# Chosen-key logits as half-height products in pairs, masks from one signed comparison, scores in 512-key units

## The reference, cut to what matters

```python
for each block of 128 queries (tile t, keys 0 .. 128*(t+1)-1):
    rel   = relu(einsum('bqjd,bkd->bqjk', qi_blk, k_idx))     # 8 index heads of width 64
    score = einsum('bqjk,bqj->bqk', rel, wi_blk)              # one score for each query and key
    _, sel = lax.top_k(score, 256)                            # 256 keys for each query, ties to the lower key
    logits = einsum('bqhd,bqnd->bhqn', q_blk, k[sel]) * 64 ** -0.5   # 4 heads of width 64, one shared k
    p = softmax(logits);  out = einsum('bhqn,bqnd->bqhd', p, v[sel])
```

## Time and profile before

| | us |
|---|---|
| median of 3 runs | 2766.08 (2763.96 to 2767.02) |
| profiled execution, time / span of the core | 2757.8 / 2756.1 |
| TensorE busy | 2467.8 (90%) |
| VectorE busy | 1202.4 (44%) |
| ScalarE busy | 914.0 (33%) |
[...]

### The profile page before, as it was taken

How to read it: one execution, slowest core, us unless ns; L and a number is a source line. 1 busy time by engine, 2 the same in 40 slices (tenths; PEclk the granted TensorE clock), 3 DMA queues, 4 the chain that set the end, 5 groups by cost and what they waited for, 6 DMA issues and landing times.

```text
span 2756.1 us, 30251 instructions
## 1 busy us (share of the span) xinstructions
PE 2467.8 (90%) x10376; PEld 1394.6 (51%) x10392; DVE 1202.4 (44%) x2802; ACT 914.0 (33%) x1882; POOL 186.3 (7%) x370
## 2 busy tenths in 40 slices
PE   6999789789999789999589996997899996999994
PEld 3565334555665444444345643455566553444442
DVE  3434468875542411111333426789655333111115
ACT  2131379554531111111122215794545211111113
POOL 0000031000000000000200001310000000000002
PEclk9999999999999889999789999999999997999996
DMA  6100001401000389999511000013010005999975
GB/s 237 43 31 25 31 13 51 120 2 47 1 11 39 148 319 359 368 364 370 195 42 52 7 25 34 19 55 107 1 47 1 26 31 230 342 360 370 366 282 206
DMA packets 105713, 370.54 MB, mean 134 GB/s; under 512 B 20759, under 2 KB 40173, under 8 KB 81005
## 3 DMA queue, kind: packets, MB, share of 16 engines
q1 hardware_dynamic: 91760, 318.54, 32.2%
q0 software_dynamic: 13824, 50.34, 4.7%
HBM read 304.42 MB, written 64.30 MB: 134 GB/s over the span
## 4 chain that ended last, share of the span: by engine, by line
PE 70%; DVE 13%; issue 8%; ACT 6%; DMA 1%; PEldq 1%; PEld 1%; POOL 1%; DVEq 0%; ACTq 0%; SPq 0%; POOLq 0%
PE bank L1191 16%; PE bank L762 9%; PE bank L1208 8%; PE bank L1116 8%; PE bank L842 5%; PE bank L751 5%; PE bank L765 5%; PE bank L874 4%; ACT group_arena L1466 3%; ACT heads_cols L1458 2%; DVE residual L2259 1%; DVE softmax_stats L1761 1%; PE bank L1045 1%; PE bank L1177 1%; PE bank L1183 1%
## 5 line engine op out<-in xcount | busy, mean ns | idle before, releaser
L762 PE MATMUL bank<-w_ring,normed_cols 128*128 128x260 f32 (+4 forms) x1280 | 433.5, 491 | 5.2 <-ACT heads_cols L1491 3.3
L762 PEld LDWEIGHTS bank<-w_ring,normed_cols 128*128 128x128 f32 x1280 | 237.1, 191 | 173.2 <-issue 154.3
L765 PE MATMUL bank<-normed_cols,w_ring 128*128 128x512 f32 x640 | 283.2, 602 | 7.4 <-ACT group_arena L1368 6.5
L751 PE MATMUL bank<-ident,group_arena 128*128 128x128 f32 (+1 forms) x1200 | 186.8, 298 | 114.2 <-DVE group_arena L1689 92.6
L1208 PE MATMUL bank<-heads_cols,group_arena 128*128 128x512 f32 x512 | 231.8, 595 | 2.8 <-DVE group_arena L2219 2.8
L1191 PE MATMUL bank<-w_ring,group_arena 128*128 128x512 f32 x512 | 229.8, 602 | 3.5 <-issue 1.8
L751 PEld LDWEIGHTS bank<-ident,group_arena 128*128 128x128 f32 (+1 forms) x1200 | 143.7, 150 | 170.1 <-issue 92.5
L1116 PE MATMUL bank<-w_ring,heads_cols 128*128 128x512 f32 x512 | 225.5, 595 | 2.0 <-DVEq L252 2.0
L1191 PE MATMUL bank<-normed_cols,group_arena 128*128 128x512 f32 x512 | 225.0, 592 | 0.0
L765 PEld LDWEIGHTS bank<-normed_cols,w_ring 128*128 128x128 f32 x640 | 122.5, 194 | 160.7 <-issue 152.0
L2219 DVE COPY group_arena<-bank 128x256 f32<-128x256 f32 x64 | 27.2, 424 | 395.4 <-PE bank L1198 395.4
(11 more groups left out here) (322 smaller groups left out, 3070.5 us busy)
## 6 DMA issues: line engine op xcount, KB each, us to landing
heads_cols<-in_expert_w_down SPq DMA_DIRECT2D x64, 1024.0 KB, 9.2
w_ring<-in_expert_w_gate SPq DMA_DIRECT2D x32, 1024.0 KB, 10.0
w_ring<-in_expert_w_up SPq DMA_DIRECT2D x32, 1024.0 KB, 14.4
normed_cols<-in_expert_w_gate SPq DMA_DIRECT2D x32, 1024.0 KB, 10.4
normed_cols<-in_expert_w_up SPq DMA_DIRECT2D x32, 1024.0 KB, 15.5
expert_rows<-group_arena SPq DMA_DIRECT2D x64, 512.0 KB, 9.3
w_ring<-in_w_in SPq DMA_DIRECT2D x6, 2048.0 KB, 9.1
expert_rows<-heads_cols SPq DMA_DIRECT2D x1, 8192.0 KB, 27.7
```

The costliest lines, as they stand in the source:

```text
L751: last = pe.transpose(bank(4 + r % 2)[0:rows, col:col + src.shape[0]], src, ident[0:src.shape[0], 0:src.shape[0]])
L762: m = pe.matmul(out[:, 0:width], HT[:, k, part * P:(part + 1) * P], w, start=(k == 0), stop=(k == K - 1))
L765: m = pe.matmul(out[0:width, :], w, HT[:, k, part * HALF:(part + 1) * HALF], start=(k == 0), stop=(k == K - 1))
```

## The change

1. `logits` for sparse attention becomes `logits_by_pair`: heads 2i and 2i+1 are multiplied together, each on its own 64 rows. For tiles 0 to 3 both lie in one bank group; for tiles 4 to 7 they take both groups, and TensorE waits for both. The second unit of a pair issues no logits.
2. `kTd_odd` goes, and with it GpSimd's three operations on keys and TensorE's wait for them.
3. `pick` starts from a sign of score minus threshold that ScalarE computes (`compare`), with its sum; VectorE marks ties (16-bit), ranks them by a scan, corrects a limit, and one operation makes `dropped(t)`, 0 or 1, which a diagonal of negative numbers `ident_neg` adds to the logits. Tile 2 is picked before the attention, and tile t+3 rather than t+2 at tile t.
4. The maximum is negated by the reduction; the scales of the logits move into the copies of q.
5. Scoring goes in 40 units of up to 512 keys, both heads of a pair at once, in alternating bank groups and halves of `rel`; the start of the search is cut into `search_count` and `search_flip`, the second one unit later. Later projections get two steps for each slot below tile 7. Of tile 7's trials still 18 are in the slots, of the `put_later` now 5 there (3 before) and 18 in rounds.

```diff
-        LATER_STEPS = [1 if t >= 4 else 2 for t, _ in SLOTS]
-        WIDEST_SLOTS = [slot for slot in range(4, len(SLOTS)) if slot not in (18, 22)]
-        WIDEST_ROUNDS = [0, 1, 2, 4] + list(range(7, 25, 2))
-        LATER_ROUNDS = [n for n in range(3, 31) if n not in WIDEST_ROUNDS]
+        UNITS = [(t, pair, c0, min(c0 + HALF, (t + 1) * P)) for t, pair in SLOTS for c0 in range(0, (t + 1) * P, HALF)]
+        LATER_STEPS = [1 if t == T - 1 else 2 for t, _ in SLOTS]
+        WIDEST_SLOTS = [slot for slot in range(5, len(SLOTS)) if slot != 22]
+        LATER_ROUNDS = [2, 3, 5, 7, 9, 12, 14, 16, 18, 20, 22] + list(range(24, 31))
+        WIDEST_ROUNDS = [n for n in range(24) if n not in LATER_ROUNDS]
...
+                    def logits_by_pair(u):
+                        _, t, heads, _ = units[u]
+                        sets = [lg.next() for _ in range(2 // len(heads))]
+                        if t >= 2 and heads[0] == 0:
+                            pe.wait_ge(mask_ready, t - 1)
+                        if sets[-1] >= 2:
+                            pe.wait_ge(lg_taken, sets[-1] - 1)
+                        outs = [PS[n % 2] for n in sets] if len(sets) == 2 else [PS[sets[0] % 2][:, i * HALF:] for i in range(2)]
+                        chunks = [(c0, min(c0 + HALF, (t + 1) * P)) for c0 in range(0, (t + 1) * P, HALF)]
+                        ts = slice(t * P, (t + 1) * P)
+                        for c0, c1 in chunks:
+                            for i, L in enumerate(outs):
+                                rows = slice(i * HD, (i + 1) * HD)
+                                pe.matmul(L[:, c0:c1], qTd[rows, heads[0] // 2, ts], kTd[rows, c0:c1], start=True,
+                                          stop=t < 2 and c1 <= t * P)
+                        for i, L in enumerate(outs):
+                            if t < 2:
+                                m = pe.matmul(L[:, ts], ident_h[:, :], masks_h[:, 0, :], start=False, stop=True)
+                            else:
+                                for c0, c1 in chunks:
+                                    m = pe.matmul(L[:, c0:c1], ident_neg[:, :], dropped(t)[:, c0:c1], start=False, stop=True)
+                            if len(sets) == 2 or i == 1:
+                                m.then_inc(lg_ready, 1)
...
-                        if kind == "dsa" and t >= 2 and heads[0] == 0:
-                            pe.wait_ge(mask_ready, t - 1)
+                        if kind == "dsa":
+                            if heads[0] % 2 == 0:
+                                logits_by_pair(u)
+                            return
...
+                def index_unit(u):
+
+                    t, pair, c0, c1 = UNITS[u]
                     n = lg.next()
...
+                    if n >= 2:
+                        pe.wait_ge(lg_taken, n - 1)
+                    for i in range(2):
+                        m = pe.matmul(PS[n % 2][:, i * HALF:i * HALF + c1 - c0],
+                                      qTi[i * 64:i * 64 + 64, pair, t * P:(t + 1) * P],
+                                      kTi[i * 64:i * 64 + 64, c0:c1], start=True, stop=True)
+                    m.then_inc(lg_ready, 1)
...
+                def relu_unit(u):
+
+                    _, _, c0, c1 = UNITS[u]
+                    n = lg.next()
+                    at, w = (n % 2) * HALF, c1 - c0
+                    act.wait_ge(lg_ready, n + 1)
+                    if n >= 2:
+                        act.wait_ge(rel_taken, n - 1)
+                    act.activation(rel[:, :, at:at + w], PS[n % 2][:, :].rearrange("p (i c) -> p i c", i=2)[:, :, 0:w],
+                                   ACT.Relu).then_inc(rel_ready, 1)
...
+                def compare(t):
+
+                    w = (t + 1) * P
+                    if t >= 4:
+                        act.wait_ge(mask_ready, t - 3)
+                    act.activation(pick_sign[:, t % 2, 0:w], scores[:, S_OFF[t]:S_OFF[t] + w], ACT.Sign,
+                                   bias=trial_bias[:, t - 2:t - 1], scale=SIGN_SCALE,
+                                   accum_out=thr[:, 0, t - 2:t - 1]).then_inc(signs_ready, 1)
+
                 def gates_and_squares(t, h):
 
+                    if t < T - 4 and h == 1:
+                        compare(t + 4)
...
-                            chain(dve.tensor_reduce(stats(tile, heads[0], m, 0), src, AX_X, ALU.max))
-                            dve.tensor_scalar(stats(tile, heads[0], m, 1), stats(tile, heads[0], m, 0), -KINDS[kind]["scale"],
-                                              None, ALU.mult).then_inc(max_ready, 1)
+                            dve.tensor_reduce(stats(tile, heads[0], m, 1), src, AX_X, ALU.max, negate=True).then_inc(max_ready, 1)
...
+                for u, (t, pair, _, c1) in enumerate(UNITS):
+                    score(u)
+                    if pair == IDX_HEADS // 2 - 1 and c1 == (t + 1) * P:
+                        finish_row(t)
+                        search_count(t)
+                    if pair == 0 and UNITS[u - 1][0] == t + 1:
+                        search_flip(t + 1)
+                search_flip(2)
...
-                chain(dve.memset(ones_row, 1.0))
+
+                chain(dve.tensor_scalar(trial_bias[:, 0:T - 2], cur, -SIGN_SCALE, None, ALU.mult))
+                dve.sem_inc(thresholds_set, 1)
...
-                        chain(dve.tensor_scalar(a, s, th, 0.0, ALU.is_gt, ALU.add, accum_out=above))
-                        chain(dve.tensor_scalar(s, s, th, None, ALU.is_equal))
+                        dve.wait_ge(signs_ready, t - 1)
+                        chain(dve.tensor_scalar(tie, sgn, 0.0, None, ALU.is_equal))
                     if part == 1:
-                        chain(dve.tensor_tensor_scan(b, ones_row[:, 0:w], s, 0.0, ALU.mult, ALU.add))
-                        chain(dve.tensor_scalar(left, above, -1.0, float(TOPK), ALU.mult, ALU.add))
+                        chain(dve.tensor_tensor_scan(rank, ones[:, 0:1].to_broadcast([P, w]), tie, 0.0, ALU.mult, ALU.add))
                     if part == 2:
-                        chain(dve.scalar_tensor_tensor(b, b, left, s, ALU.is_le, ALU.mult))
-                        chain(dve.tensor_tensor(a, a, b, ALU.add))
+                        chain(dve.tensor_tensor(left, rank[:, w - 1:w], excess, ALU.subtract))
+                        chain(dve.tensor_scalar(left, left, 0.5, float(TOPK - w // 2), ALU.mult, ALU.add))
                     if part == 3:
-                        dve.tensor_scalar(chosen(t), a, -NEG, NEG, ALU.mult, ALU.add).then_inc(mask_ready, 1)
+                        dve.scalar_tensor_tensor(dropped(t), rank, left, sgn, ALU.is_gt, ALU.is_gt).then_inc(mask_ready, 1)
```

More of the change, by code:

```diff
@@ L345, in trunk @@
         kTd = g(14336, SEQ)
-        kTd_odd = g(15360, SEQ)
         qTi = g(0, 4, SEQ)
@@ L1436, in _ @@
                     for half in range(2):
-                        take(copy_to(qTd[:, b, half * HALF:(half + 1) * HALF]))
+                        take(copy_to(qTd[:, b, half * HALF:(half + 1) * HALF], scale=HD ** -0.5))
                 for which in range(2):
@@ L1494, in _ @@
                 i = 0
-                for slot in range(len(SLOTS)):
-                    relu_pair(slot)
+                for u, (t, pair, _, c1) in enumerate(UNITS):
+                    relu_unit(u)
+                    if c1 < (t + 1) * P:
+                        continue
+                    slot = SLOTS.index((t, pair))
                     done = sum(LATER_STEPS[:slot])
@@ L1543, in gates_and_squares @@
                         act.activation(rstd2[:, :], rstd2[:, :], ACT.Sqrt).then_inc(root_ready, 1)
+                act.wait_ge(thresholds_set, 1)
+                for t in range(2, 4):
+                    compare(t)
                 attend("dsa", extra=gates_and_squares)
@@ L1553, in take_q_k @@
                 def take_q_k(t):
-                    take(copy_to(qTm[0:DQ, :, t * P:(t + 1) * P], rows=DQ))
+                    take(copy_to(qTm[0:DQ, :, t * P:(t + 1) * P], rows=DQ, scale=DQ ** -0.5))
                     take(copy_to(kTm[0:DQ, :, t * P:(t + 1) * P], rows=DQ))
@@ L2066, in _ @@
                     dve.wait_ge(stage_out[i], 16 * N_STAGED // 4)
+                for part in range(4):
+                    pick(2, part)
                 attend("dsa", extra=pick_and_norm)
```

165 lines of the change are left out of this document (65 added, 100 removed).

## The result

The changed kernel takes 2785.09 us (median of 4 runs, 2784.7 to 2787.21), the kernel before 2766.55 (4 runs, 2763.96 to 2769.36). The ratio is 1.0067, 95% interval 1.0053 to 1.0082: 18.5 us slower. Forecast was 2788, and slower with a chance of 0.71.

What follows compares the result with a forecast made beforehand. TensorE bounds the two other attentions, ScalarE the search, the order of waits scoring and sparse attention. -4.2 - 0.6 - 0.4 + 9.8 + 6.6 - 0.3 = +10.9 a layer, +21.8 on 2757.8, plus 8.3: 2788 us; range 2757 to 2802.

Steps and rivals of the forecast that it cites:

- Scoring: Scoring stage: alternating banks end TensorE and ScalarE's turn-taking; earlier first trial, shorter trial stretch and tail; -4.2 us a layer.
- the rival: Scoring nears VectorE's bound because GpSimd decides quicker; stage under 85 us, -6 a layer overall, 2754 us, chance 0.18.
- Search: Search stage: one `put_later` less on ScalarE, -0.6 us a layer (0 to -1).
- Masks and maxima up to tile 5's opening: Sparse attention's early tiles, VectorE the limit: cheaper picks bring tile 5's opening to 558.9, -0.4 us a layer (-3 to +3).
- Joint logits: Sparse attention, tiles 5 to 7: cheaper products, but pairs need both bank groups, nothing computed ahead; +9.8 us a layer (+4 to +13).
- half clock: Sparse attention: TensorE's granted clock drops behind its pauses before pairs' logits; four pairs at 1.65 us, +6.6 us a layer.
- Rest: Two other attentions follow TensorE, so their shorter maxima give only the first units; -0.3 us a layer.
- no half clock: Sparse attention: TensorE's pauses slightly shorter than thought, so no slow clock; +4.3 us a layer, 2775 us, chance 0.17.
- Faster: Scoring near VectorE's bound, -11 us a layer; attention +5 without the clock's cost; -6 a layer, 2754 us, chance 0.18.
- Gain and loss cancel: Whole kernel: no net change within 5.5 us (0.2%), 2766 us, chance 0.10.
- Signs change tables: ScalarE in sparse attention: each of four signs costs up to two table loads; +5 us a layer on top, 2798, chance 0.05.

Runs made afterwards that it cites:

- e7: Changed kernel plus 32 unread products of 128 columns into the outputs' bank before each pair's logits from tile 4 on: 2760.59 us, 0.9998 of the kernel before.
- e5: Changed kernel with the kernel before's logits put back (full height, one head at a time, keys split by GpSimd): 2724.81 us, 0.9871 of the kernel before.
- e10: Changed kernel with ScalarE's squares for both heads of a pair moved behind the second exponential: 2772.97 us, 1.0024 of the kernel before.
- e6: e5 with the old maxima, VectorE negating each maximum in an instruction of its own: 2727.74 us, 0.9878 of the kernel before.
- e4: Changed kernel plus nine unread 512-column products into a transposes' bank before pairs' logits from tile 4's second pair on: 2781.72 us, 1.0053 of the kernel before.
- e1: Changed kernel with pairs kept only for tiles 0 to 3, later heads' half-height logits issued singly into their own bank group: 2741.2 us, 0.9907 of the kernel before.

## Why the prediction was right

The sign and the main cause were right. The sizes, per layer (predicted, then measured in the traces; e7's and e5's where named):

- **Scoring, -4.2 and -7.4.** (The three terms given add up to -4.1.) The step that failed is the pace of the trials. The first trial was placed at 332.5 and came at 332.78. But 64.7 us were taken from first to last, and it was 60.8. I had taken GpSimd's decision between two trials as a fixed pace, though I had put "the decisions become quicker when the rows are split" into the rival. The decision itself did not become quicker (its four instructions take 1.5 us on average before and 1.6 after, from 334 to 400 us); what became shorter is GpSimd's wait for ScalarE's next trial, 2.1 us before and 1.7 after. I take it that less stands ahead of the trials in ScalarE's order; that was not tried by itself. The rival's mark of 85 us was not reached (87.7).
- **Search, -0.6 and -0.6.** As predicted.
- **Masks and maxima up to tile 5's opening, -0.4 and +2.1.** The opening came at 553.42 in place of 559.29, 5.9 earlier, where scoring and search alone give 8.0. Up to tile 4's logits the forecast held: counted without these 8.0 they came at 541.2 (533.22 in the trace), and 542.0 was forecast, with the sign of tile 7 and two table loads of 1.28 us ahead of them. The step that failed is tile 4's first pair. From its opening to the next I had 9.7 us, and it was 12.2; the second pair took 8.0 for 7.2. Two things lie in that first pair, and no run separates them (it takes 12.4 us in e7 and 12.1 in e10). It opens after a pause of 5.79 us, and the granted clock behind is 0.52 (533.22 to 537.90), with logits of 2.50 us where the second pair's take 1.35. And the second head's maximum, ready to start when the masks end at 536.9, stands in VectorE's order behind a step that waits for the forgetting sums from ScalarE:

```profile
542.05 0.43 DVE L2041 TENSOR_SCALAR group_arena<-group_arena 128x1024 f16<-128x1024 f16 x1 [1.87 <-ACT forget L1530]
...
542.51 0.83 DVE L1789 TENSOR_REDUCE softmax_stats<-bank 128x1 f32<-128x640 f32 x1
...
545.41 1.35 PE L831 MATMUL bank<-group_arena 64*128 64x512 f32 x8 [1.51 <-ACTq L1367]
```

  The kernel before has the same wait, but there it holds up one head and not a pair. This term was also hiding something: with the pairs gone (e5) the same masks and maxima bring 4.9 us up to tile 5's opening (546.34) and 3.4 behind it, 8.3 in all (16.3 less scoring and search). VectorE was the limit of tiles 4 and 5, as the prediction said, but the joint logits put another wait in its place, so that nothing of the relief was left.
- **Joint logits, +9.8, and half clock, +6.6: 16.4 together, and 20.5** from tile 5's opening to the last values. The joint part is right where the clock is full. In e7 both pairs of tile 5 took 17.8 us (17.4 predicted), both of tile 6 19.1 (19.4), the first of tile 7 9.35 (9.4), and the rest to the last values 19.7 where it was 18.9 before (0.8 more, as predicted): +9.8 in sum. What was mis-sized is the clock. No run shows the +6.6 that the sum has for it, which was my estimate of four pairs at 1.65 us; in its place the runs showed +10.7 by the same rows (tile 5 20.95 to 17.8, tile 6 22.3 to 19.1, tile 7's first pair 12.17 to 9.35, the rest 21.2 to 19.7). Three of the four pairs (the second of tile 5, both of tile 6) cost 1.57 to 1.64, but tile 7's first cost 2.8, and two that I did not count, tile 5's first and tile 7's last, cost 1.6 and 1.5: behind each of the six openings, after pauses of 2.1 to 3.0 us, some products were slow (behind 553.42 the values took 2.21 us for 20, where they take 1.31 in e7 at a granted clock of 1.00).
- **Rest, -0.3 and about -1.8.** The attention ended 14.7 us later and the out projection began 12.9 later (822.91 for 810.05). The difference lies in the two other attentions, 155.5 us long where they were 157.3; the old maxima (e6) give 0.5 of it back, the remainder was not tried.

Sum: +10.9 predicted and +12.8 measured, against 12.9 at the out projection in the trace; 21.8 for two layers against 27.3 between the two traces. The medians differ by 18.5. The 8.3 us that I added for the distance of the profiled execution from its median applied to the kernel before and not to the changed one. So it was partly luck that the forecast of 2788 came within 3 us: sums too small by 5.5 and an offset too large by 8.3 went against each other.

The rivals: *no half clock* is refuted by the windows of 0.69 and 0.58. Its condition, pauses a little shorter than thought, would not have been enough: in e10 pauses of 1.86 and 2.01 us are followed by granted clocks of 0.66 and 0.72, and one of 2.04 by 1.00. *Faster* came halfway with its scoring (-7.4, between the forecast's -4.2 and its -11), but its attention of +5 without the clock's cost was not seen: with filler (e7) scoring and search at -8.0 and the attention at +12.1 leave the yardstick 4.1 above the kernel before's. *Gain and loss cancel* is out by 18.5 us against its 5.5. *Signs change tables* is refuted: the sign at 526.66 has no table load ahead of it, the load at 528.04 belongs to the logarithm of the forget gates and the one at 530.29 to the exponential after it. Between the loads at 506.87 and 528.04 the trace has none, and four signs lie there between exponentials (510.00, 513.89, 519.22 and 526.66); the first of them:

```profile
509.43 0.36 ACT L1362 ACTIVATE heads_cols<-bank,softmax_stats 128x128 f32<-128x128 f32 x1
...
510.00 0.83 ACT L1538 ACTIVATE group_arena<-group_arena 128x640 f16<-128x640 f32 x1
...
510.99 0.37 ACT L1362 ACTIVATE heads_cols<-bank,softmax_stats 128x128 f32<-128x128 f32 x1
```

So the exponential behind this sign needed no load, and that the load of the earlier trace rows comes from the sign is not shown.

## What to carry to other kernels

Before two units are joined so that they share an engine, count the buffers: if the joined unit takes all of them, nothing is computed ahead any more, and every engine's work between two joined units lies end to end. Here a pair's logits and masks fell from 4.3 us to 2.9 at full clock (tile 7), and the pairs as a whole rose by 3.4 to 4.3. A change made of independent parts should be timed in parts: this one hid 16 us a layer of gain (1.2% of the kernel) under 31 of loss, and its net looks like a small failure. And where TensorE must wait for 2 to 3 us, look at the granted clock behind the wait: moving another engine's work out of the gap was worth 12 us here, and useless products at its start 21 to 24. Read the clock instead of judging by the length of the wait: after pauses of 1.9 to 2.0 us either level was found.

## What the runs showed of the hardware

- Useless products in the pauses made the kernel 24.5 us faster by the medians and 21 by twice the yardstick (e7 against the changed kernel): 32 products of 128 columns in 1.95 us at the start of each pause kept the granted clock at 1.00 behind the six openings of tiles 5 to 7, where it had been 0.58 to 0.70. Filler that starts 2.4 us into the pause did not help (e4: 3.62 us for eight products of 512 columns, 0.45 each, where four masks of the same width take 1.04 in e7).
- A pause of TensorE's of some 2 us was followed by either clock level: by granted clocks of 0.66, 0.72 and 0.63 after 1.86, 2.01 and 2.11 us and by 1.00 after 2.04 in e10, and by 1.00 after 1.97 in e4 (587.92, filler in 1.89 us).
- A half-height product beside another one is cheap (eight of 512 columns in 1.99 us in e7, where four at full height with a mask between them take 2.10 before), but alone, between full-height ones, a chunk of 512 columns with its mask takes 1.37 us (e1) in place of 1.08 (e5). In e1 the rows of the weight loads show why this may be: the engine that loads weights sits idle for 0.76 and 0.23 us around each change of height, where between the full-height products of the kernel before it is 0.24 and 0.33. That the change of height is the cause was not tried by itself.

```profile
587.00 0.29 PEld L864 LDWEIGHTS bank<-group_arena 64*128 64x128 f32 x2 [0.17 <-issue]
588.05 0.10 PEld L867 LDWEIGHTS bank<-group_arena,ident_neg 128*128 128x128 bf16 x1 [0.76 <-issue]
588.37 0.29 PEld L864 LDWEIGHTS bank<-group_arena 64*128 64x128 f32 x2 [0.23 <-issue]
```

- The tie test on 16-bit signs takes 0.37 us for 896 columns and 0.43 for 1024, where the comparison in float32 took 0.69 (kernel before, 550.65) and 0.76.
